# Sixteen gate weight units of block 2's two FFNs computed as seven block products each

## What is computed

```python
def swiglu(x, w_in, w_out):
    gate, up = jnp.split(x @ w_in, 2, axis=-1)
    return (jax.nn.silu(gate) * up) @ w_out

h = h + 0.5 * swiglu(rms_norm_2(h, ffn1_norm[i]), ffn1_w_in[i], ffn1_w_out[i])
...
h = h + 0.5 * swiglu(rms_norm_2(h, ffn2_norm[i]), ffn2_w_in[i], ffn2_w_out[i])
```

## Time and profile before

| | us |
|---|---|
| median of 3 runs | 2156.07 (2155.74 to 2157.17) |
| profiled execution, its own time | 2155.7 |
| its span in the trace | 2153.9 |
| TensorE busy in the span | 2144.9 |
| GpSimd, VectorE, ScalarE busy | 947.4, 982.3, 754.6 |

### The profile page before, as it was taken

The page is one execution under the profiler, slowest core; times in us unless marked ns, Lnnn a source line. Parts: engine busy times, 40 slices in busy tenths (PEclk is TensorE's granted clock), DMA queues, the critical chain, the costliest instruction groups (busy, mean ns, idle before and its releaser), DMA issues.

```text
span 2153.9 us, 31464 instructions
## 1 busy us (share of the span) xinstructions
PE 2144.9 (100%) x12580; PEld 1853.2 (86%) x12580; DVE 982.3 (46%) x1478; ACT 754.6 (35%) x1022; POOL 947.4 (44%) x735
## 2 busy tenths in 40 slices
PE   9999999999999999999999999999999999999999
PEld 8897999999999887888888788888788888888888
DVE  5244454279888208322200719661876442222017
ACT  4133455342222216322212415651346332222134
POOL 3322223446555544455544541054432555555444
PEclk9999999999999999999999999999999999999999
DMA  4321111212222323222222221123220222222222
GB/s 167 104 77 62 60 59 60 99 62 96 97 97 95 107 94 122 100 97 97 97 98 98 98 99 69 40 79 137 79 79 21 98 98 97 97 97 98 98 98 98
DMA packets 31950, 195.19 MB, mean 91 GB/s; under 512 B 3968, under 2 KB 4480, under 8 KB 10096
## 3 DMA queue, kind: packets, MB, share of 16 engines
q1 hardware_dynamic: 26784, 182.86, 23.6%
q10 hardware_dynamic: 5072, 11.00, 1.6%
HBM read 189.48 MB, written 4.23 MB: 90 GB/s over the span
## 4 chain that ended last, share of the span: by engine, by line
PE 90%; DVE 3%; POOL 2%; issue 2%; ACT 1%; DMA 1%; SPq 0%; POOLq 0%; DVEq 0%; ACTq 0%
PE ps L2597 76%; POOL wlo L743 2%; PE ps L3247 2%; PE ps L2665 2%; PE ps L3462 1%; PE ps L3446 1%; PE ps L3382 1%; PE ps L3329 1%; DMA raw<-wstream 1%; PE ps L2913 1%; PE ps L2840 1%; PE ps L2875 0%; PE ps L2936 0%; PE ps L3427 0%; PE ps L2972 0%
## 5 line engine op out<-in xcount | busy, mean ns | idle before, releaser
L743 POOL TENSOR_TENSOR wlo<-raw,whi 128x512 fp32r<-128x512 f32 (+2 forms) x724 | 942.0, 1333 | 1176.2 <-ACT whi L839 1089.6
L839 ACT CAST whi<-raw 128x2048 fp32r<-128x2048 f32 x160 | 305.7, 1911 | 816.5 <-PE ps L2597 759.5
L2597 PE MATMUL ps<-x2hi,whi 128*128 128x512 f32 (+1 forms) x1152 | 451.7, 392 | 0.4 <-DVE x2lo L1631 0.4
L2597 PE MATMUL ps<-x2hi,wlo 128*128 128x512 f32 (+1 forms) x1152 | 445.2, 386 | 0.0
L2597 PE MATMUL ps<-x2lo,whi 128*128 128x512 f32 (+1 forms) x1152 | 444.9, 386 | 0.0
L2597 PE MATMUL ps<-xhi,whi 128*128 128x256 f32 (+2 forms) x1304 | 263.2, 283 | 0.6 <-DVE vb L1746 0.3
L2597 PE MATMUL ps<-xlo,whi 128*128 128x256 f32 (+2 forms) x1304 | 260.7, 281 | 0.0
L2597 PE MATMUL ps<-xhi,wlo 128*128 128x256 f32 (+2 forms) x1304 | 260.7, 281 | 0.0
L2597 PEld LDWEIGHTS ps<-x2hi,whi 128*128 128x128 f32 x1152 | 216.5, 188 | 47.3 <-issue 3.8
L2597 PEld LDWEIGHTS ps<-x2lo,whi 128*128 128x128 f32 x1152 | 216.5, 188 | 44.2 <-issue 1.9
L2597 PEld LDWEIGHTS ps<-x2hi,wlo 128*128 128x128 f32 x1152 | 216.4, 188 | 43.9
(11 more groups left out here) (509 smaller groups left out, 2804.1 us busy)
## 6 DMA issues: line engine op xcount, KB each, us to landing
raw<-wstream SPq DMA_DIRECT2D x170, 1024.0 KB, 4.8
ncb<-c_rows ACTq DMA_DIRECT2D x8, 256.0 KB, 3.6
ple_rows<-ple_out ACTq DMA_DIRECT2D x4, 512.0 KB, 3.5
bias<-bias_rows ACTq DMA_DIRECT2D x8, 256.0 KB, 4.3
ple<-ple_rows ACTq DMA_DIRECT2D x4, 512.0 KB, 5.5
out_dram<-outb SPq DMA_DIRECT2D x8, 256.0 KB, 2.5
h_all<-h SPq DMA_DIRECT2D x1, 792.0 KB, 10.5
h_all<-h SPq DMA_DIRECT2D x2, 264.0 KB, 7.3
```

What stands on the lines that cost most here:

```text
L743: return nc.gpsimd.tensor_tensor(wlo[b][:, cols], raw[b][:, cols], whi[b][:, cols].bitcast(F32), ALU.subtract)
L839: nc.scalar.copy(whi[b][:], raw[b][:]).then_inc(sig("hi_done"), 1)
L2597: ins = mm(dst, w[slot][:, cols], xx(tok), start=first and p_ == 0, stop=last and p_ == 2, skip_group_check=True)
```

## The change

In each of the two FFNs, gate units of pairs 3 to 10 (`SEVEN_FROM` = 3, so 8 units each) are no longer multiplied as they stand. A unit is cut in four blocks A11, A12, A22, A21 (512 input features x 128 gate columns each; the host lays them out so), and the activations in four blocks B11, B12, B21, B22 (512 features x 256 tokens). The 2x2 block product is made by Winograd's scheme, with seven block products in place of eight. A block product is 4 chunks x 3 matmuls of 128x256. That takes

- four weight sums per unit, S1 = A21 + A22, S3 = A11 - A21, S2 = S1 - A11, S4 = A12 - S2, made by VectorE from `raw[0]` into `ssum`; ScalarE casts all four to `whi[0]`, GpSimd makes their low parts in `wlo[0]`;
- the high and low parts of the plain blocks A11, A12, A22, in `sxh` (ScalarE) and `sxl` (GpSimd);
- four activation sums per FFN, `tsum`, with `thi` and `tlo`;
- additions of the seven products on VectorE (`gate_of_parts`), in place of `by_fold`.

Since these need normalised activations, each FFN now normalises them into `xn` after pair 0 and rewrites `x2hi` and `x2lo` chunk by chunk while the value unit of pair 1 and the gate unit of pair 2 are multiplied (`by_chunks`). The gated hidden values stay in fp32 in `hid` until the last pair, and `hhi`, `hlo` are made then. `down` waits for them unit by unit.

```diff
+def seven_units(w):
+    units = pairs_up(w)
+    for i in range(2 * SEVEN_FROM, FC, 2):
+        v = units[i].reshape(P, KC, 2, P)
+        quarters = [v[:, 0:4, 0], v[:, 4:8, 0], v[:, 4:8, 1], v[:, 0:4, 1]]
+        units[i] = np.ascontiguousarray(np.concatenate(quarters, axis=1)).reshape(1, P, UT * P)
+    return units
...
+            def low_sevens(unit0, layer):
+                first = unit0 // 2 + SEVEN_FROM
+                with pool.Fori(first, first + SEVENS) as i:
+                    pool.wait_ge(sig("a_hi"), i + (since("a_hi", layer) + 1 - first))
+                    for q in range(3):
+                        cols = slice(q * BANK, (q + 1) * BANK)
+                        nc.gpsimd.tensor_tensor(sxl[:, cols], raw[0][:, cols], sxh[:, cols].bitcast(F32), ALU.subtract)
+                    pool.wait_ge(sig("hi_done"), i * 2 + 1)
+                    for q in range(4):
+                        cols = slice(q * BANK, (q + 1) * BANK)
+                        ins = nc.gpsimd.tensor_tensor(wlo[0][:, cols], ssum[:, cols], whi[0][:, cols].bitcast(F32),
+                                                      ALU.subtract)
+                    ins.then_inc(sig("lo_done"), 1)
+                    pool.wait_ge(sig("hi_done"), i * 2 + 2)
+                    for q in range(3):
+                        low_part(1, q)
+                    low_part(1, 3).then_inc(sig("lo_done"), 1)
...
+                def plain_hi(i):
+                    b = unit0 % 2
+                    act.wait_ge(sig("raw_ready0"), (i + (unit0 // 2 + 1)) * 16)
+                    act.wait_ge(sig("unit_done"), i * 2 + (unit0 + 1))
+                    nc.scalar.copy(sxh[:], raw[b][:, 0:3 * BANK]).then_inc(sig("a_hi"), 1)
+                def sums_hi(i):
+                    act.wait_ge(sig("s_sum"), i * 4 + (since("s_sum", layer) - 4 * SEVEN_FROM + 8))
+                    nc.scalar.copy(whi[0][:], ssum[:]).then_inc(sig("hi_done"), 1)
...
+                hi_of(unit0 + 4)
+                for k in range(KC):
+                    act.wait_ge(sig("xn_ready"), since("xn_ready", layer) + k + 1)
+                    if k < KC - 1:
+                        act.wait_ge(sig("chunk_free"), since("chunk_free", layer) + k + 1)
+                    else:
+                        act.wait_ge(sig("unit_done"), unit0 + 4)
+                    nc.scalar.copy(x2hi[:, k, :], xn[:, k, :]).then_inc(sig("xn_hi"), 1)
+                hi_of(unit0 + 5)
+                act.wait_ge(sig("gate_ready"), ready + 2)
                 act.wait_ge(sig("prod"), done + 1)
-                nc.scalar.copy(hhi[:, 0:2, :], cvl[:]).then_inc(sig("hid_hi"), 1)
-                with act.Fori(1, FC // 2) as i:
-                    hidden_act(i, False, unit0, done, silu)
-                    hidden_hi(i, unit0, done)
+                silu(1)
+                act.wait_ge(sig("t_sum"), since("t_sum", layer) + 4)
+                for t in range(4):
+                    nc.scalar.copy(thi[:, t], tsum[:, t]).then_inc(sig("t_hi"), 1)
+                plain_hi(2)
+                act.wait_ge(sig("prod"), done + 2)
+                nc.scalar.activation(gact[:], pair(bank(0, 2)), ACT.Silu).then_inc(sig("gate_act"), 1)
+                sums_hi(2)
+                hi_of(unit0 + 7)
+                with act.Fori(SEVEN_FROM, FC // 2 - 1) as i:
+                    plain_hi(i)
+                    silu_first(i)
+                    sums_hi(i)
+                    silu_rest(i)
+                    weights_hi(1, i + (unit0 // 2 + 1))
...
+                def weight_sums(i):
+                    a11, a12, a22, a21 = [raw[0][:, q * BANK:(q + 1) * BANK] for q in range(4)]
+                    s1, s2, s3, s4 = [ssum[:, q * BANK:(q + 1) * BANK] for q in range(4)]
+                    summed = since("s_sum", layer) - 4 * SEVEN_FROM + 4
+                    dve.wait_ge(sig("raw_ready0"), (i + (unit0 // 2 + 1)) * 16)
                     dve.wait_ge(sig("unit_done"), i * 2 + (unit0 + 1))
-                    if not first:
-                        dve.wait_ge(sig("gate_act"), i + done)
-                    by_fold(cg[:], bank(2 * gate, 2)).then_inc(sig("gate_ready"), 1)
-                    dve.wait_ge(sig("unit_done"), i * 2 + (unit0 + 2))
-                    dve.wait_ge(sig("hid_lo"), i + done)
-                    by_fold(cvl[:], bank(2 * value, 2)).then_inc(sig("val_ready"), 1)
-                    dve.wait_ge(sig("val_ready"), i + (done + 1))
-                    dve.wait_ge(sig("gate_act"), i + (done + 1))
-                    vec.tensor_tensor(cvl[:], cvl[:], gact[:], ALU.mult).then_inc(sig("prod"), 1)
-                    dve.wait_ge(sig("prod"), i + (done + 1))
-                    dve.wait_ge(sig("hid_hi"), i + (done + 1))
-                    vec.tensor_tensor(hlo[:, bass.ds(i * 2, 2), :], cvl[:],
-                                      hhi[:, bass.ds(i * 2, 2), :].bitcast(F32), ALU.subtract
+                    add(s1, a21, a22, ALU.add).then_inc(sig("s_sum"), 1)
+                    add(s3, a11, a21, ALU.subtract).then_inc(sig("s_sum"), 1)
+                    dve.wait_ge(sig("s_sum"), i * 4 + (summed + 1))
+                    add(s2, s1, a11, ALU.subtract).then_inc(sig("s_sum"), 1)
+                    dve.wait_ge(sig("s_sum"), i * 4 + (summed + 3))
+                    add(s4, a12, s2, ALU.subtract).then_inc(sig("s_sum"), 1)
+                def gate_of_parts(i):
+                    parts = since("part_done", layer) - 3 * SEVEN_FROM
+                    dve.wait_ge(sig("part_done"), i * 3 + (parts + 1))
+                    vec.tensor_copy(psum1[:], bank(0)[:, 0:HALF]).then_inc(sig("p1_read"), 1)
+                    dve.wait_ge(sig("p1_read"), i + (since("p1_read", layer) - SEVEN_FROM + 1))
+                    step.up(add(wsum[:], bank(5)[:, 0:HALF], psum1[:], ALU.add))
+                    dve.wait_ge(sig("part_done"), i * 3 + (parts + 2))
+                    step.wait()
+                    twice = wsum[:].rearrange("p (a n) -> p a n", a=1).to_broadcast([P, 2, HALF])
+                    step.up(add(vsum[:], pair(bank(1)), twice, ALU.add))
+                    dve.wait_ge(sig("gate_act"), i + done)
+                    step.wait()
+                    step.up(add(cgf[:, 3 * HALF:], bank(1)[:, HALF:], vsum[:, 0], ALU.add))
+                    dve.wait_ge(sig("part_done"), i * 3 + (parts + 3))
+                    add(pair(cgf[:, HALF:3 * HALF]), pair(bank(4)), vsum[:], ALU.add).then_inc(sig("gate_ready"), 1)
...
+                folded_gate(0)
+                folded_value(0)
+                folded_product(0)
+                for k in range(KC):
+                    vec.scalar_tensor_tensor(out=xn[:, k, :], in0=hview(k), scalar=cv[:, gain + k:gain + k + 1],
+                                             in1=fold[:], op0=ALU.mult, op1=ALU.mult).then_inc(sig("xn_ready"), 1)
+                folded_gate(1)
+                for k in range(KC):
+                    dve.wait_ge(sig("xn_hi"), since("xn_hi", layer) + k + 1)
+                    vec.tensor_tensor(x2lo[:, k, :], xn[:, k, :], x2hi[:, k, :].bitcast(F32), ALU.subtract
+                                      ).then_inc(sig("xn_lo"), 1)
                 if layer == 1:
                     dve.wait_ge(sig("p_in"), 5 * 16)
-                with dve.Fori(1, FC // 2) as i:
-                    one(i, False)
+                folded_value(1)
+                b11, b12 = xn[:, 0:4, 0:HALF], xn[:, 0:4, HALF:]
+                b21, b22 = xn[:, 4:8, 0:HALF], xn[:, 4:8, HALF:]
+                t1, t2, t3, t4 = [tsum[:, t] for t in range(4)]
+                add(t1, b12, b11, ALU.subtract).then_inc(sig("t_sum"), 1)
+                add(t3, b22, b12, ALU.subtract).then_inc(sig("t_sum"), 1)
+                dve.wait_ge(sig("t_sum"), since("t_sum", layer) + 1)
+                add(t2, b22, t1, ALU.subtract).then_inc(sig("t_sum"), 1)
+                dve.wait_ge(sig("t_sum"), since("t_sum", layer) + 3)
+                add(t4, b21, t2, ALU.subtract).then_inc(sig("t_sum"), 1)
+                folded_product(1)
+                t_low(0)
+                t_low(1)
+                weight_sums(2)
+                t_low(2)
+                t_low(3)
+                product(2)
+                with dve.Fori(SEVEN_FROM, FC // 2 - 1) as i:
+                    step.enter(i - SEVEN_FROM, 3)
+                    gate_of_parts(i)
+                    weight_sums(i)
+                    product(i)
+                step.leave(SEVENS - 1)
+                gate_of_parts(FC // 2 - 1)
+                for i in range(5):
+                    hidden_low(i)
...
+                for i in range(5, FC // 2):
+                    hidden_low(i)
...
+                def product(weights, q, tokens, dst, more=False, last=True):
+                    (w_hi, w_lo), (x_hi, x_lo) = weights, tokens
+                    for k in range(4):
+                        cols = slice(q * BANK + k * P, q * BANK + (k + 1) * P)
```

(103 more changed lines are left out.)

94 lines of the change are left out of this document (79 added, 15 removed).

## The result

The changed kernel takes **2171.75 us** (2169.34 to 2173.39, 4 runs), the kernel before beside it 2156.01 (2155.74 to 2157.17, 4 runs): ratio 1.0072, 95% interval 1.006 to 1.0084, slower by 15.7 us. The forecast was 2172, range 2160 to 2180. The profiled execution took 2171.9, its span is 2170.1: 16.2 us above the span before, 2153.9, and this difference is what I account for.

What follows compares the result with a forecast made beforehand. TensorE, busy in all of the span, was taken to bound the kernel. Terms: 7.0 + 18.8 + 3.0 - 12.6 = +16.2 us on the profiled 2155.7 gave 2171.9, stated as 2172, range 2160 to 2180.

Steps and rivals of the forecast that it cites:

- What is taken away: Gate units on TensorE: 10.08 us in place of 10.87, 0.79 less, times 16 units, 12.6 us less.
- The rival with 0.1132 us for a matmul: TensorE's narrow matmuls take half a wide one's time, not 0.120: 9.1 us less, 2163; chance 0.03.
- The loop's wait: TensorE waits for GpSimd's seven subtractions, pairs 4 to 10: 0.5 us each, 14 times, 7.0 us more.
- S: Start of a gate unit's last matmul; the loop's preparations for the next gate unit are timed from it.
- The rival with larger waits, 1.0 each: Loop: register and semaphore instructions add 0.5 us per pair, 14 times: 2179; chance 0.17.
- The heads: Start of each FFN: TensorE waits for first seven-product operands, 1.9 and 9.8 us in first, 7.1 in second; 18.8 together.
- The rivals with half or with nothing of the heads: FFN heads: half as long, 9.4 us less, 2161, chance 0.12; or hidden, only loop waits staying, 2150.1, chance 0.06.
- The clock: After the head waits TensorE runs at half pace for some 3 us: 1.5 us lost per FFN, 3.0 us.
- At no cost: FFN's end (`hhi`, `hlo`, `down`) and the loads: covered by other work, adding nothing.

Runs made afterwards that it cites:

- experiment 6: Changed kernel with `SEVEN_FROM` = 4 and VectorE instead of GpSimd making the low part of S4: 2147.42 us.
- experiments 1 and 2: Against the changed kernel, first: S2 and S4 subtract an idle PSUM bank, 2163.10 us; second: VectorE, not GpSimd, makes S4's low part, 2163.12 us.
- Experiment 5: Changed kernel with `SEVEN_FROM` = 4, pair 3 multiplied as in the kernel before, head casts and weight sums moved with it: 2154.77 us.
- experiments 3 and 7: Changed kernel with filler matmuls before the first seven-product unit: 3, 72 in first FFN, 52 in second, 2169.51 us; 7, the 52 alone, 2168.32 us.

## Why the prediction was right, step by step

Terms against the trace of the changed kernel:

| step | predicted us | measured us |
|---|---|---|
| sixteen units on TensorE | -12.6 | -12.0 |
| the loop's waits, 14 times | +7.0 | +7.0 |
| waits in the heads | +18.8 | +17.0 |
| half pace after them | +3.0 | +4.0 |
| sum, on the spans | +16.2 | +16.0 (16.2 in all) |

- **What is taken away.** Without waits a pair is 20.98 long (experiment 6), before it was 96 x 0.2264 = 21.73: 0.75 for a unit and not 0.79. The 54 narrow matmuls of the earlier trace rows were the right row: they give 10.08 for a unit, the trace 20.98 - 10.87 = 10.11. The rival with 0.1132 us for a matmul is out.
- **The loop's wait.** 21.48 - 20.98 = 0.50 each, as summed, and experiments 1 and 2 show its place. Link by link from S, here 920.23: the cast begins after 0.32 (0.37), takes 1.49 (1.48 by interpolation), GpSimd follows 0.07 later (0.08) with 9.43 (8.76 + 0.65 = 9.41), TensorE 0.14 after it (0.05): 11.45 against 11.39. The rival with larger waits, 1.0 each, is out. That it came so near is partly luck: the wait is what is left of 11.4 less 11.0.
- **The heads.** TensorE's starts are 1.59, 9.24 and 6.88 us apart where 0.23 is normal: 1.36, 9.0 and 6.65 of wait, against 1.9, 9.8 and 7.1. In the second FFN the list was right to 0.45 us: TensorE could have gone on at 1813.8, the casts end 4.7 us before that and GpSimd 6.5 after; I had 4.25 and 6.95. In the first, GpSimd ended at 908.7 and not at 909.8: the first `x2lo` was done 0.4 sooner (the eight `xn` took 9.54 and not 9.9), from there to the end of `tsum` I had 0.3 too much, and for ScalarE's casts another 0.3 (5.3 and not 5.6). (That TensorE is "4.4 us nearer" there is a slip: by the rows it is 13.1 - 9.8 = 3.4; the sum doesn't use it.) Experiment 5 shows the cause of the two long waits: with one more pair of cover both are gone. The wait of 1.36 for `x2lo` stays in every version. The rivals with half or with nothing of the heads are out.
- **The clock.** 22.82 - 21.48 = 1.3 in the first FFN, 24.19 - 21.48 = 2.7 in the second, against 1.5 each. Right in kind, shown by experiments 3 and 7, and short by a quarter. The longer rest had the smaller price, and after equal rests of 6.49 the count of slow matmuls was 28 in the second FFN of the changed kernel and 13 in the first FFN of experiment 7: the length of a rest doesn't give its price here, and what does is open.
- **At no cost.** Nothing of the FFN's end, `down` or the loads shows up: the four terms leave 0.2 of the 16.2.

The misses nearly cancel: 1.8 too much in the heads, against 0.6 too much taken away and 1.0 too little for the clock. That the total came within 0.2 us is luck; that it came out near 16 is the mechanism.
